# One-core hybrid trunk: indexer, key and value tiles regrouped around the attention loop

## What is computed

```python
proj = h @ w_in                      # q (16 heads x 64), c_kv (256), q_idx (8 x 64), k_idx (64), w_idx (8)
c_kv = rms_norm(c_kv, kv_norm)
score = sum_h w_idx[h] * relu(q_idx[h] @ k_idx.T)       # per query block of 128, causal by chunks of 64
top_idx = top_k(score, 128)                             # the keys that a query may see
logits = (q w_uk) . c_kv[top_idx] / 8 ;  p = softmax(logits)
out = (p @ c_kv[top_idx]) w_uv ;  x = x + g_m * (out @ w_out)
```

## Time and profile before

| | us |
|---|---|
| three runs | 3582.94, 3587.43, 3588.46 |
| median | 3587.43 |
| span of the profiled execution | 3584.2 |
| attention, from the first input tile to the last output tile | about 44 to 361 |
| attention loop, first logits to the last head pair's low part | 201.7 to 321.3 |
| mean granted TensorE clock | 0.990 of full speed |

### The profile page before, as it was taken

How to read it: one execution, slowest core, us unless ns; L and a number is a source line. 1 busy time by engine, 2 the same in 40 slices (tenths; PEclk the granted TensorE clock), 3 DMA queues, 4 the chain that set the end, 5 groups by cost and what they waited for, 6 DMA issues and landing times.

```text
span 3584.2 us, 62733 instructions
## 1 busy us (share of the span) xinstructions
PE 3463.3 (97%) x19978; PEld 3144.9 (88%) x19978; DVE 2604.0 (73%) x4761; ACT 1767.7 (49%) x3216; POOL 1120.5 (31%) x852
## 2 busy tenths in 40 slices
PE   7988999999999999998999999899999999999998
PEld 5545799999999999997776688689999999999997
DVE  2654668579996888886887644585669996888886
ACT  3354445557884333335774133345557875333333
POOL 2100442434441222222664002343444442222221
PEclk8999999999999999999999999999999999999999
DMA  7654245799999999993457452235698999999995
GB/s 241 210 166 141 73 140 172 235 331 333 381 377 370 359 345 350 344 345 105 156 172 209 131 161 78 80 114 174 198 342 302 375 376 365 368 348 347 345 349 192
DMA packets 519774, 914.08 MB, mean 255 GB/s; under 512 B 70256, under 2 KB 359152, under 8 KB 511216
## 3 DMA queue, kind: packets, MB, share of 16 engines
q1 hardware_dynamic: 445936, 644.23, 52.4%
q0 software_dynamic: 73728, 268.47, 21.0%
HBM read 782.54 MB, written 130.02 MB: 255 GB/s over the span
## 4 chain that ended last, share of the span: by engine, by line
PE 87%; ACT 5%; DMA 3%; DVE 3%; issue 1%; SPq 0%; POOL 0%; DVEq 0%; ACTq 0%; POOLq 0%
PE bank L736 11%; PE bank L738 11%; PE bank L737 11%; PE bank L808 10%; PE bank L810 10%; PE bank L809 10%; PE bank L784 5%; PE bank L446 3%; PE bank L956 2%; PE bank L965 1%; PE bank L539 1%; PE bank L747 1%; DMA w_ring<-b_w_in 1%; PE bank L1030 1%; PE bank L1032 1%
## 5 line engine op out<-in xcount | busy, mean ns | idle before, releaser
L736 PE MATMUL bank<-hx,hl 128*128 128x384 f32 (+1 forms) x2304 | 798.0, 346 | 0.8 <-POOL hl L1512 0.8
L738 PE MATMUL bank<-hx,hl 128*128 128x384 f32 (+1 forms) x2304 | 785.7, 341 | 0.0
L737 PE MATMUL bank<-hx,hl 128*128 128x384 f32 (+1 forms) x2304 | 785.5, 341 | 0.0
L808 PE MATMUL bank<-W,hl 128*128 128x384 f32 x2048 | 688.8, 336 | 6.2 <-DVE W L2558 6.2
L810 PE MATMUL bank<-W,hl 128*128 128x384 f32 x2048 | 688.4, 336 | 0.0
L809 PE MATMUL bank<-W,hl 128*128 128x384 f32 x2048 | 688.3, 336 | 0.0
L1535 POOL DMA_INDIRECT rows<-p_v,erow x256 | 262.0, 1024 | 850.8 <-DVE xtok L2565 828.8
L1535 POOL DMA_INDIRECT rows<-p_u,erow x256 | 356.6, 1393 | 405.1 <-DVE rows L2491 367.2
L1840 ACT ACTIVATE hl<-hT 128x1024 fp32r<-128x1024 f32 x272 | 287.8, 1058 | 358.1 <-PE bank L810 303.4
L1840 ACT ACTIVATE hl<-w_ring 128x1024 fp32r<-128x1024 f32 x272 | 287.6, 1058 | 342.7 <-PE bank L810 304.7
L736 PEld LDWEIGHTS bank<-hx,hl 128*128 128x128 f32 x2304 | 434.6, 189 | 10.5 <-POOL hl L1512 1.0
(11 more groups left out here) (355 smaller groups left out, 5411.0 us busy)
## 6 DMA issues: line engine op xcount, KB each, us to landing
w_ring<-p_u_t SPq DMA_DIRECT2D x128, 512.0 KB
hT<-p_u_t SPq DMA_DIRECT2D x128, 512.0 KB
w_ring<-p_v SPq DMA_DIRECT2D x128, 512.0 KB
hT<-p_v SPq DMA_DIRECT2D x128, 512.0 KB
act_scratch<-hT SPq DMA_DIRECT2D x256, 192.0 KB
g_scratch<-gst SPq DMA_DIRECT2D x48, 1024.0 KB
gg<-g_scratch SPq DMA_DIRECT2D x64, 768.0 KB
ua<-act_scratch SPq DMA_DIRECT2D x256, 192.0 KB
```

The lines of the kernel that those rows point to most:

```text
L736: nc.tensor.matmul(bank[s][:, c:], hi, hx[:, 0, k, c:], start=(k == 0), stop=False)
L737: nc.tensor.matmul(bank[s][:, c:], hi, hx[:, 1, k, c:], start=False, stop=False)
L738: mm = nc.tensor.matmul(bank[s][:, c:], lo, hx[:, 0, k, c:], start=False, stop=(k == KD - 1))
L808: nc.tensor.matmul(bank[j][:, P:], hi, W[:, s, 0, :], start=first, stop=False)
```

## The change

1. The indexer pairs move closer together. Query tile 7 now holds all eight pairs of query blocks 0 and 1, one behind every k; tile 8 the four pairs of block 2, tile 9 those of block 3, behind every second k as before.
2. The key tiles move between query tiles: three behind tile 10, two behind 11, three behind 12, into banks 5, 6, 7 in turn. They are written to `hT`, which is free by then; the old place of `kT` is called `wide`.
3. The value tiles move into the loop: two behind the logits of each of steps 0 to 3, and their evacuations behind ScalarE's exponentials of the step.
4. The halves of `ada_w` come in steps 4, 5, 7, 8, ... 25, 26 (two of every three), where they came in steps 0 to 15.
5. ScalarE copies the transposes of step m-3 *before* the exponentials of step m.
6. Weight tiles 2 to 5 of `a_w_out` are loaded into `wide`, ahead; tiles 6 and 7 into `w_ring` once tiles 0 and 1 are split. All are issued ahead of the late chunks. `out_high(0)` and `out_high(1)` move to steps 28 and 30.

```diff
+INDEXED = [[(0, 0), (0, 1), (0, 2), (0, 3), (1, 0), (1, 1), (1, 2), (1, 3)], [(2, 0), (2, 1), (2, 2), (2, 3)],
+           [(3, 0), (3, 1), (3, 2), (3, 3)]]
+KEYS_AT = [0, 0, 0, 1, 1, 2, 2, 2]
+VALUE_STEPS = KD // 2
+HALF_AT = [VALUE_STEPS + m for m in range(3 * HALVES // 2) if m % 3 < 2]
+OUT_AHEAD = 4
...
+        def out_raw(m):
+
+            if 2 <= m < 2 + OUT_AHEAD:
+                return wide[:, 2 * m - 4:2 * m - 2, :].rearrange("p a (b c) -> p (a b) c", c=P)
+            return w_ring[:, m % 2, :, :]
...
+                def indexed(m, k):
+                    pairs = INDEXED[m]
+                    every = KD // len(pairs)
+                    if k % every == every - 1:
+                        two_indexers(*pairs[k // every])
+
+                def keys_tile(j):
...
+                    b = 5 + j % 3
+                    take(b)
                     for r in range(2):
                         mm = nc.tensor.matmul(bank[b][:, :], w_ukv[:, 0, r, j * P:(j + 1) * P], ckvT[:, r, :],
...
                 for m in range(KD):
-                    in_tile(7 + m, m % 2, between=(lambda j, m=m: two_indexers(m, j)) if m < TT else None)
+                    in_tile(7 + m, m % 2, between=(lambda k, m=m: indexed(m, k)) if m < len(INDEXED) else None)
                     ada_rows(4 + m)
                     if m > 0:
                         ada_columns(3 + m)
...
+                    for j in range(KD):
+                        if KEYS_AT[j] == m - len(INDEXED):
+                            keys_tile(j)
+                ada_columns(11).then_inc(psum_full[3], 1)
...
-                    if 0 < m < HALVES:
-                        half_columns(m - 1)
-                    if m < HALVES:
-                        half_rows(m)
-                    if m == HALVES:
-                        half_columns(m - 1).then_inc(sem("halves_turned"), 1)
+                    if m < VALUE_STEPS:
+                        values_tile(2 * m)
+                        values_tile(2 * m + 1)
+                    if m - 1 in HALF_AT:
+                        mm = half_columns(HALF_AT.index(m - 1))
+                        if m - 1 == HALF_AT[-1]:
+                            mm.then_inc(sem("halves_turned"), 1)
+                    if m in HALF_AT:
+                        half_rows(HALF_AT.index(m))
...
                 def load_out(m):
-                    sp.dma_start(slot(m % 2), a_w_out[:, m * P:(m + 1) * P].rearrange("(k p) c -> p k c", p=P)
-                                 ).then_inc(sem(f"raw_loaded{m % 2}"), 16)
+
+                    nth = t.turn(f"raw{m % 2}")
+                    if m < 2:
+                        sp.wait_ge(sem(f"split_done{m % 2}"), nth + 1)
+                    elif m >= 2 + OUT_AHEAD:
+                        sp.wait_ge(sem(f"split_done{m % 2}"), nth + 1 - OUT_AHEAD // 2)
+                    sp.dma_start(out_raw(m), a_w_out[:, m * P:(m + 1) * P].rearrange("(k p) c -> p k c", p=P)
+                                 ).then_inc(out_loaded(m)[0], 16)
...
-                for m in range(2, 4):
+                for m in range(2, KD):
                     load_out(m)
-                sp.wait_ge(psum_full[6], marks["heads"][6] + KD)
-                for m in range(4, KD):
-                    load_late(m - 4)
-                    load_out(m)
+                sp.wait_ge(psum_full[6], marks["heads"][6] + VALUE_STEPS + KD)
+                for c in range(LATE):
+                    load_late(c)
...
                 for m in range(PAIR_STEPS + LAG + 1):
+                    if LAG <= m < PAIR_STEPS + LAG:
+                        turned(m - LAG)
                     if m < PAIR_STEPS:
                         exponentials(m)
-                    if LAG <= m < PAIR_STEPS + LAG:
-                        turned(m - LAG)
...
-                    if m < HALVES:
+                    for j in (2 * m, 2 * m + 1) if m < VALUE_STEPS else ():
+                        evac(6 + j % 2, vA[:, j // 2, (j % 2) * T:(j % 2 + 1) * T])
+                    if m in HALF_AT:
                         evac(7, half_part[:, :], bank[7][:, 0:HALF])
-                    if m in (HALVES + 1, HALVES + 3):
-                        out_high((m - HALVES) // 2)
+                    if m in (HALF_AT[-1] + 2, HALF_AT[-1] + 4):
+                        out_high((m - HALF_AT[-1]) // 2 - 1)
```

More of the change, by code:

```diff
@@ L198, in hybrid_trunk @@
         stage_.close()
-        kT = sb("kT", [P, KD, T], where=part)
+        wide = sb("wide", [P, KD, T], where=part)
         stage_ = ExitStack()
@@ L404, in gate_loaded @@
             s, nth = (g - 2) % 8, (g - 2) // 8
-            name, before = (("x_loaded", 32), ("small_loaded", 48), ("narrow_loaded", 16), ("ukv_loaded", 32),
+            name, before = (("x_loaded", 48), ("small_loaded", 64), ("narrow_loaded", 32), ("ukv_loaded", 48),
                             ("act_loaded0", 16 * (NK // 4)), ("act_loaded1", 16 * (NK // 4)),
@@ L418, in hybrid_trunk, with out_loaded, late_loaded @@
         late_bank = (3, 4, 5, 2)
+        def out_raw(m):
+            if 2 <= m < 2 + OUT_AHEAD:
+                return wide[:, 2 * m - 4:2 * m - 2, :].rearrange("p a (b c) -> p (a b) c", c=P)
+            return w_ring[:, m % 2, :, :]
+        def out_loaded(m):
+            if 2 <= m < 2 + OUT_AHEAD:
+                name, before = (("x_loaded", 32), ("small_loaded", 48), ("narrow_loaded", 16), ("ukv_loaded", 32))[m - 2]
+                return sem(name), before
+            return sem(f"raw_loaded{m % 2}"), None
+        def late_loaded(c):
+            if c < 2:
+                return sem(f"half_loaded{c}"), 16 * (HALVES // 2 + 1)
+            return sem(f"ada_loaded{c - 2}"), 16 * 5
         def ada_slot(n):
-            return {2: qT, 3: kT}[n][:, :, :] if n in (2, 3) else ada_ring[:, n % 2, :, :]
+            return {2: qT, 3: wide}[n][:, :, :] if n in (2, 3) else ada_ring[:, n % 2, :, :]
         block = ctx.enter_context(nc.Block())
@@ L543, in in_tile @@
                             mm.then_inc(psum_full[b], 1)
-                        if between and k % 2 == 1:
-                            between(k // 2)
+                        if between:
+                            between(k)
                 in_tile(0, 0, by_block=True)
@@ L576, in two_indexers @@
                                          ).then_inc(psum_full[b], 1)
+                def indexed(m, k):
[4 more added lines that the diff above has]
+                def keys_tile(j):
+                    if j == 0:
+                        pe.wait_ge(sem("ukv_loaded"), 32)
+                        pe.wait_ge(sem("ckv_ready"), 1)
+                    b = 5 + j % 3
+                    take(b)
+                    for r in range(2):
+                        mm = nc.tensor.matmul(bank[b][:, :], w_ukv[:, 0, r, j * P:(j + 1) * P], ckvT[:, r, :],
+                                              start=(r == 0), stop=(r == 1))
+                    mm.then_inc(psum_full[b], 1)
                 take(3)
                 for m in range(KD):
-                    in_tile(7 + m, m % 2, between=(lambda j, m=m: two_indexers(m, j)) if m < TT else None)
+                    in_tile(7 + m, m % 2, between=(lambda k, m=m: indexed(m, k)) if m < len(INDEXED) else None)
                     ada_rows(4 + m)
@@ L583, in attention, with values_tile @@
                         ada_columns(3 + m)
[L585 to L598, removed]
+                    for j in range(KD):
+                        if KEYS_AT[j] == m - len(INDEXED):
+                            keys_tile(j)
+                ada_columns(11).then_inc(psum_full[3], 1)
+                def values_tile(j):
+                    tt, c, b = j // 2, j % 2, 6 + j % 2
                     take(b)
@@ L614, in logits @@
                         nc.tensor.matmul(bank[b][:, 0:(tt + 1) * P], qT[r:r + HD, hp, tt * P:(tt + 1) * P],
-                                         kT[r:r + HD, hp, 0:(tt + 1) * P], start=True, stop=True
+                                         hT[r:r + HD, hp, 0:(tt + 1) * P], start=True, stop=True
                                          ).then_inc(psum_full[b], 1)
@@ L638, in half_columns @@
                 def half_columns(n):
[L639 removed]
+                    pe.wait_ge(psum_free[7], base[7] + VALUE_STEPS + n + 1)
                     for c in range(2):
@@ L696, in late_rows @@
                 for c, b in enumerate(late_bank):
-                    pe.wait_ge(sem(f"half_loaded{c % 2}"), 16 * (HALVES // 2 + 2 + c // 2))
+                    loaded, before = late_loaded(c)
+                    pe.wait_ge(loaded, before + 16)
                     take(b)
@@ L1762, in attention @@
                 for m in range(KD):
[L1763 to L1769, removed]
+                    for tt, j in INDEXED[m] if m < len(INDEXED) else ():
+                        for n in (IH * tt + 2 * j, IH * tt + 2 * j + 1):
+                            N = (tt + 1) * P
+                            b = 5 + n % 3
+                            full(b)
```

(6 more changed lines are left out.)

13 lines of the change are left out of this document (7 added, 6 removed).

## The result

The changed kernel takes 3565.95 us (median of 7 runs, 3564.45 to 3581.2), the kernel before 3588.39 (median of 7, 3582.94 to 3601.8). Their ratio is 0.9934, interval 0.9916 to 0.9953: faster by 22 us, 0.66%. Forecast was 3565.5, a gain of 21.9. That the median lies only 0.45 us from the forecast is luck in part: four of the seven runs lie between 3564.45 and 3565.95, the other three between 3576.81 and 3581.2, and six later runs of the same kernel have a median of 3574.3 (ratio 0.9939).

A forecast was written before the change was run, and what follows sets the result against it. TensorE was full ahead of the loop; in it, a chain round the engines held the steps and loads held the halves. Terms -15.4 + 1.5 - 6.7 - 1.3 = -21.9, from 3587.4 to 3565.5 us, range 3558 to 3574.

The forecast's parts named there:

- Value tiles out of the front: Ahead of the loop: first logits follow the last key tile and ada_columns(11), 15.5 us go, 0.1 stays; term -15.4 us.
- Key tiles: Between query tiles: same matmuls on the same engine, so 0 us; a late weight load is covered by three key tiles.
- Pairs: Query tile 7: closer index pairs stall TensorE behind a slow score multiplication for 1.5 us, bounds 0 and 5.
- Selection earlier: VectorE's mask and modulations end about 183.8 instead of 190.67, ahead of first logits at 187.8; otherwise VectorE late by 3.
- The loop: First logits to last low part: 112.8 us instead of 119.5, so -6.7; pieces: steps 0-3, 4-26, waits, step 27 on.
- the rival of locks and pairs: Both GpSimd low parts block VectorE, +2.7 us, and index pairs stall at their upper bound, +3.5: 3571.7 us; chance 0.08.
- the rival in which clock and locks go well: No low part meets a multiplication, no 1.2 GHz stretch, third steps covered: loop 108 us, time 3560.5; chance 0.16.
- The chain holds the loop: Reversed ScalarE order gives TensorE nothing, value tiles fill only steps 0 to 3, loop stays 119.5 us: 3572; chance 0.13.
- the term that names it: Step 27 on: copies ahead of exponentials shrink TensorE's waits, a four-step cycle going from 11.0 to 8.7 us: -2.3.
- Slow loads: Loads of halves landing later than 7.7 us cost 7 us per further us; loss from 10.8, 3596 at 12; chance 0.03.
- my signs of being wrong: TensorE waiting for loads or banks in steps 4-26, first logits after 190, or loop clock below 0.9 over a few us.
- Output weights ahead: Behind the loop: last high part no longer waits for its load, sum of squares ends sooner, root follows its table; -1.3 us.

The follow-up runs named there:

- The experiment: Changed kernel with the value tiles back ahead of the loop: 254.07 us from query tile 7 to the last square, against 251.59 and 250.75 in the changed kernel's two profiles.

## Why the prediction was right, point by point

**The total.** Direction and size are right, and so are the terms ahead of the loop and behind it. That the sum of the stretch comes within 0.2 us is luck: the profile before has one stretch at 1.2 GHz more, against the second profile of the changed kernel the gain is 22.96, and inside the loop two errors cancel.

**Value tiles out of the front, -15.4.** Right: the front fell by 14.04, with the 1.35 us stall of the pairs in it, 15.4 without. That steps 0 to 3 pay for it I had as 17.4; it is 17.65, TensorE without a gap. But I listed the two in different parts, and so the text reads as if this were the gain. The experiment says 2.5 to 3.3 us; the loop without value tiles lasts 100.72.

**Key tiles, 0.** Right.

**Pairs, +1.5.** Right in cause and size: 1.35 in the wait, 1.69 when undone. The bound of 5 would have needed stalls at every pair; none came behind that one (TensorE's waits for the relu in tile 7 are this single row).

**Selection earlier, "VectorE would be late by 3" without it.** This step fails. Its end was forecast near 183.8 and was 182.1, in a profile 1.49 us ahead at tile 7, so this is right, and without it VectorE is late. But I priced lateness as if every us of it reached TensorE; behind the first logits it has 3.70 us of value tiles, and of 4.0 us of lateness 2.3 reach it (steps 0 to 27, 86.29 against 83.99, neither with a stretch at 1.2 GHz or a wait for a half). So closer pairs cost 1.69 us and save 2.3: next to nothing, where I had them at 1.5 of cost for 3 of gain.

**The loop, -6.7 as 17.4 + 67.5 + 1.5 + 26.4.** Measured 17.65, 67.20 (203.84 to 271.04, forecast 69.0) and 28.13 (271.04 to 299.17). Errors of -1.8 and +1.7 cancel. In steps 4 to 26 the third step's hole is covered better than I allowed: in 203.84 to 275.73 TensorE is busy 71.10 of 71.89. In the last piece 27 to 31 took 9.14, not 8.7, and the end is longer by 2.8 than before. As far as the runs split that, 0.7 is the low clock, 0.7 the low parts (moved, they give it back), and 0.8 comes with the order alone (16.95 against 16.19); 0.6 stays open. I had let one of two low parts meet VectorE, and both did. VectorE's and GpSimd's timeline around them in the changed kernel:

```profile
278.74 2.35 POOL L1528 TENSOR_TENSOR aw<-w_ring,aw 128x1024 fp32r<-128x1024 f32 x1 [114.19 <-ACT aw L1855]
...
279.18 1.94 DVE L2343 TENSOR_SCALAR nmx<-mx 128x2 f32<-128x2 f32 x1
...
285.26 2.86 DVE L2353 TENSOR_SCALAR prob<-prob,rinv 128x384 f32<-128x384 f32 x2
285.43 2.47 POOL L1528 TENSOR_TENSOR aw<-w_ring,aw 128x1024 fp32r<-128x1024 f32 x1 [4.33 <-ACT aw L1855]
```

A multiplication of two columns, 0.17 us otherwise, took 1.94 beside the first; a pair of normalisations 2.86 beside the second, like the 2.98 of the earlier trace rows; with that low part gone it takes 0.75. The exponentials of step 29 and the copies behind them wait for the first, and TensorE for those copies, 1.57 us before 282.87. Then it ran its sixteen outputs in 4.06 us at a granted clock of 0.50, the 1.2 GHz level, where they take 2.38 at full clock. That this fall of the clock comes from the wait isn't shown: the same wait has no fall behind it in three other kernels. The exclusive lock of the Trainium skill (SBUF — State Buffer, section "SBUF: two separate sides") agrees with both pairs of rows. But the 2.7 us that the sum would have been worse by it did not come: the last piece is 1.7 over its forecast for all causes together, and moving the low parts gives back 0.7.

**The other rivals.** Both locks did block, as the rival of locks and pairs says, but for less than its price, and the pairs did not add theirs; the clock did fall, so the rival in which clock and locks go well didn't come about either.

**The chain holds the loop (3572).** Wrong, and the two experiments on the order say so: 10.8 us with it undone, 10.4 with it alone, at least 8 and 7 of them if the low clock is taken out. My argument for the forecast, that the value tiles fill the holes, was the weaker half; the copies' place in ScalarE's order carries it, and the term that names it (-2.3, four steps' worth) is where I gave it least. By its own measure, 11.01 to 9.14 in steps 27 to 31, it was right at -1.9; the rest was hidden in the 67.5, as work of TensorE without waits.

**Slow loads.** The median half load of the changed loop takes 5.5 us from issue to landing. The one that TensorE waited 0.79 us for was issued at 215.71 and took 6.68: it was wanted at 222.44 - 0.79 = 221.65, 5.94 us after its issue and not the 7.7 of the forecast. So the margin of that rival was thinner than I had it. By the letter this is one of my signs of being wrong, TensorE waiting for a load in steps 4 to 26; it is this one wait, the second profile has none, and the loads kept up.

**Output weights ahead, -1.3.** Right: 1.52 in the profile (1.15 in the second), 1.04 to 1.41 when undone.

Added up, undoing one thing at a time from the changed kernel gives 10.8 (order) + 7.6 (spread) + 2.5 (value tiles) + 1.4 (loads) - 1.0 (pairs) = 21.3 of 22.1. The agreement is closer than the terms are, for stretches at 1.2 GHz sit in order and spread (8 and 5 us at the least); that the parts don't interact isn't shown. What is shown is that the order and the spread are most of it: 18.3 of 22.1 by themselves, and 15 of 19 with the low clock taken out.

## What to carry to other kernels

Before holes are filled with work from elsewhere, ask what makes them: here one swap in ScalarE's order closed 7 to 10 us, and of the 14 us of matmuls that went into the loop three quarters or more were paid there. A term won in one stage and paid in the next belongs in one line of the sum. Where whole times scatter by more than an edit is worth, compare a stretch between two instructions that both kernels have, profile the same kernel twice to learn what that stretch can tell, and look in each profile for the places where the granted clock is low before you give a difference to an edit.

## What I had not expected of the hardware

TensorE's matmuls from about 3025 us on had a pitch longer by 1.8% in two of thirteen profiles (568 in 100 us instead of 578), at a granted clock printed as 1.00 in both; 548.9 us instead of 539.0 each time for the last 3000 matmuls. It may be most of the difference between the runs near 3565 and those near 3577, which the runs, without a profile each, can't show. Its cause stays open.

A VectorE multiplication of 128x2 elements waits for a GpSimd instruction as a large one does: 1.94 us for 0.17.

The granted clock fell to 0.50 for 3 to 4 us in step 0 in three of thirteen profiles, with TensorE at work without a wait for more than 90 us ahead of it; within some 2 us behind the wait of 1.56 to 1.57 us in step 31 it fell in four profiles and stayed at 1.00 in three others.
